# A streaming encoder layer: two more plain up-projection blocks, one weight cast moved to ScalarE, t1 kept in DRAM, and the closing norm's sums of x on VectorE

## What is computed

```python
h = x * (1 + sc2) + sh2
u = h @ w_up + b_up                     # 1024 -> 2 x 2816
ctx = concatenate([conv_buf, u], axis=1)
uc = conv_b + sum(conv_w[j] * ctx[:, j:j + T] for j in range(3))
a, g = split(uc, 2, axis=-1)
f = (a * gelu(g)) @ w_down              # 2816 -> 1024
x = layer_norm(ALPHA * x + g2 * f, ln2_w, ln2_b)
```

## Time and profile before

| | |
|---|---|
| median of 3 runs | 1892.29 us (1892.24 to 1895.44) |
| the profiled execution | 1895.71 us, its span 1893.9 us |
| TensorE busy | 1813.9 us, 96% of the span |
| VectorE, GpSimd, ScalarE busy | 1130.8, 862.4, 608.7 us |
| mean granted TensorE clock | 0.981 of full speed |
| chain that ended last | TensorE 84%, VectorE 6%, GpSimd, ScalarE and DMA 2% each |

### The profile page before, as it was taken

How to read it: one execution, slowest core, us unless ns; L and a number is a source line. 1 busy time by engine, 2 the same in 40 slices (tenths; PEclk the granted TensorE clock), 3 DMA queues, 4 the chain that set the end, 5 groups by cost and what they waited for, 6 DMA issues and landing times.

```text
span 1893.9 us, 30909 instructions
## 1 busy us (share of the span) xinstructions
PE 1813.9 (96%) x12255; PEld 1737.0 (92%) x12255; DVE 1130.8 (60%) x2002; ACT 608.7 (32%) x1375; POOL 862.4 (46%) x605
## 2 busy tenths in 40 slices
PE   7999999999999999999999996889999999999984
PEld 6999888888999999899999996889999999999983
DVE  4837875773322324364345869675676668666687
ACT  3213444433222323342111685122222222322345
POOL 0332212212222222133336357297778778877851
PEclk9999999999999999999999998899999999999997
DMA  9443321114334334265333001011111111101112
GB/s 389 167 145 107 120 85 69 57 57 136 97 107 125 123 107 121 84 230 182 125 125 102 12 12 49 23 46 45 45 46 68 39 53 45 68 23 68 45 34 83
DMA packets 78903, 173.44 MB, mean 92 GB/s; under 512 B 9300, under 2 KB 42452, under 8 KB 78632
## 3 DMA queue, kind: packets, MB, share of 16 engines
q1 hardware_dynamic: 55112, 119.63, 18.8%
q10 hardware_dynamic: 23648, 51.84, 7.7%
HBM read 139.21 MB, written 32.24 MB: 91 GB/s over the span
## 4 chain that ended last, share of the span: by engine, by line
PE 84%; DVE 6%; POOL 2%; ACT 2%; DMA 2%; DVEq 2%; issue 2%; ACTq 0%; SPq 0%; POOLq 0%
PE acc L607 37%; PE px L889 12%; PE acc L889 7%; PE px L935 6%; PE acc L935 4%; PE px L854 2%; PE px L678 1%; PE acc L854 1%; PE px L878 1%; PE px L707 1%; PE px L690 1%; PE px L704 1%; PE px L780 1%; PE px L779 1%; PE px L778 1%
## 5 line engine op out<-in xcount | busy, mean ns | idle before, releaser
L607 PE MATMUL acc<-x_hilo_a,w_hilo 128*128 128x352 f32 x4032 | 664.3, 324 | 2.6 <-ACT x_c L1037 1.7
L607 PEld LDWEIGHTS acc<-x_hilo_a,w_hilo 128*128 128x128 f32 x4032 | 643.1, 188 | 10.8 <-issue 10.0
L485 POOL CAST w_hilo<-w_raw 128x1024 fp32r<-128x1024 f32 x73 | 84.8, 1162 | 732.7 <-PE acc L607 624.8
L510 POOL TENSOR_TENSOR w_unit<-w_raw,w_unit 128x512 fp32r<-128x512 f32 x116 | 171.5, 1478 | 70.6 <-ACT w_unit L1371 61.7
L487 POOL TENSOR_TENSOR w_hilo<-w_raw,w_hilo 128x1024 fp32r<-128x1024 f32 x73 | 189.0, 2589 | 5.8
L935 PE MATMUL px<-ffn_act,w_unit 128*128 128x352 f32 x900 | 152.0, 324 | 0.6 <-issue 0.5
L935 PEld LDWEIGHTS px<-ffn_act,w_unit 128*128 128x128 f32 x900 | 145.6, 189 | 1.6 <-issue 1.4
L889 PE MATMUL px<-x_hilo_a,w_unit 128*128 128x264 f32 x1128 | 145.2, 284 | 0.2 <-POOL w_unit L510 0.2
L1774 DVE SCALAR_TENSOR_TENSOR c_state<-c_state,stage,px 128x257 f32<-128x257 f32 x36 | 17.4, 482 | 206.9 <-PE px L780 206.9
L889 PEld LDWEIGHTS px<-x_hilo_a,w_unit 128*128 128x128 f32 x1128 | 140.5, 188 | 0.3 <-issue 0.3
L889 PE MATMUL px<-h_sums,w_unit 128*128 128x264 f32 x828 | 109.2, 287 | 3.5 <-POOL w_unit L510 3.5
(11 more groups left out here) (319 smaller groups left out, 3037.4 us busy)
## 6 DMA issues: line engine op xcount, KB each, us to landing
w_raw<-in_w_panels SPq DMA_DIRECT2D x141, 512.0 KB, 3.3
z_spill<-stage ACTq DMA_DIRECT2D x41, 528.0 KB, 2.7
adaT_ring<-in_w_adaT SPq DMA_DIRECT2D x32, 512.0 KB, 4.5
stage<-z_spill ACTq DMA_DIRECT2D x20, 528.0 KB, 4.8
ada_ring<-in_w_ada SPq DMA_DIRECT2D x16, 512.0 KB, 13.3
zc<-z_spill SPq DMA_DIRECT2D x8, 1024.0 KB, 9.8
x_c<-in_x SPq DMA_DIRECT2D x8, 528.0 KB, 14.9
x_c<-in_x ACTq DMA_DIRECT2D x8, 528.0 KB, 4.0
```

The lines of the kernel that those rows point to most:

```text
L485: nc.gpsimd.tensor_copy(to[:, 0, :], raw[:, s, :]).then_inc(w_hi, 1)
L510: nc.gpsimd.tensor_tensor(to[:, 1, :], src, to[:, 0, :].bitcast(F32), ALU.subtract).then_inc(w_ready, 1)
L607: last = mm(acc[:, n, 0:NW], whl[:, slot, wi, k * P:(k + 1) * P], rhs[:, xi, k, n * NW:(n + 1) * NW], start=(k == 0 and j == 0), stop=(k = ...
```

## The change

- SINGLES takes in pi 3: eight plain blocks instead of six, and the first pair is pi 4 (PAIR0 = 4). Its order of terms is that of the others.
- The unit slots are handed out by the order in which the terms read them: a new unit takes the slot whose holder is read first (`unit_places`, UNIT_PREV). Of a pair, S4 now takes S2's slot (before: S1's), the next A11 takes S1's.
- ScalarE also casts the high half of A11 for each pair that doesn't follow a down-projection (even pi from 6 to 20, and 21), at the point of its queue between `x_take` of the pair before and `up_tap`. GpSimd waits for it on `a_hi`.
- t1 is no longer formed from XA. `sums_full` leaves it in h_full; ScalarE's queue stores it to DRAM after each `sums_high`, and loads it into XA's low part after the eighth block is taken. From the third on, `h2_full` waits until the first two stores have landed.
- The scaling of XC moves from VectorE to ScalarE, one row block at a time, with a semaphore on which VectorE's first down rows wait.
- The order of ScalarE's and VectorE's queues at the seam is another: `up_take(2)` stands ahead of the last `h2_full`.
- The closing norm's sums of x are formed by VectorE with `ln_add`, ahead of each `ln_add_square`; the loop at the end of GpSimd's program is gone.

```diff
-SINGLES = ((0, 0), (0, 1), (1, 0), (1, 1), (2, 0), (2, 1))
+SINGLES = tuple((pi, r) for pi in range(4) for r in range(2))
-PAIR0 = 3
+PAIR0 = 4
...
-        order += [("p", j, 1), ("p", j + 1, 0), ("d", j, 0), ("d", j, 1)]
+        order += [("p", j, 1)] * (j > 1) + [("p", j + 1, 0), ("d", j, 0), ("d", j, 1)]
...
-UNIT_SLOT = {unit: r % NUNIT for r, unit in enumerate(UNIT_RING)}
+def unit_places():
+
+    reads = [(item, part) for item in ITEMS[NSING:] for part in (terms(2 * item[1] + item[2]) if item[0] == "p" else (0, 1))]
+    slot, prev, held = {}, {}, {}
+    for r, unit in enumerate(UNIT_RING):
+        if r < NUNIT:
+            slot[unit], prev[unit] = r, None
+        else:
+            prev[unit] = min(held.values(), key=reads.index)
+            slot[unit] = slot[prev[unit]]
+        held[slot[unit]] = unit
+    return slot, prev
...
+        def after_down(pi):
+            return pi % 2 == 1 and PAIR0 < pi < 2 * FF - 2
+
+        def plain_parts(pi):
+            return ("A12", "A22") if pi == PAIR0 or after_down(pi) else ("A11", "A12", "A22")
...
-                if unit[1] in ("A12", "A22"):
-                    pool.wait_ge(a_hi, 2 * (2 * unit[0][1] + unit[0][2] - PAIR0) + (1 if unit[1] == "A12" else 2))
+                pi = 2 * unit[0][1] + unit[0][2]
+                if unit[1] in plain_parts(pi):
+                    pool.wait_ge(a_hi, high_of(pi, unit[1]))
...
+            split(P_FFN + 6)
+            split(P_FFN + 7)
...
-            for n in range(NT):
-                cols = slice(n * NW, (n + 1) * NW)
-                for m in range(1, KT - 2 if n == NT - 1 else KT):
-                    pool.wait_ge(r_rdy, rank(1, m, n) + 1)
-                    if m > 1:
-                        pool.wait_ge(s1_add, (KT - 1) * (NT + n) + m - 1)
-                    nc.gpsimd.tensor_tensor(lsum2[:, 0, cols], XC[:, 0, cols] if m == 1 else lsum2[:, 0, cols], XC[:, m, cols], ALU.add)\
-                      .then_inc(s1_add, 1)
...
+            def t1_store(kt):
+                act.dma_start(io["t1"][kt], hb[:, kt % 2, 0, 0:HN]).then_inc(ffn_dma, 16)
+
+            def t1_load(kt):
+                act.dma_start(XA[:, 1, kt, HN:T].bitcast(F32), io["t1"][kt]).then_inc(ffn_dma, 16)
...
             def h2_full(kt):
                 if kt >= 2:
                     act.wait_ge(ts_lo, kt - 1)
                     act.wait_ge(t34_lo, kt - 1)
+                    act.wait_ge(ffn_dma, 16 * 3)
...
+            def residual_scale(k):
+                A(XC[:, k, :], XC[:, k, :], ACT.Identity, scale=der[:, 4, k:k + 1], bias=der[:, 5, k:k + 1]).then_inc(xc_rdy, 1)
...
             sums_high(1)
+            up_take(1, 2)
             h2_full(2)
-            up_take(1, 2)
-            h2_full(3)
             up_tap(0, 1)
-            sums_high(2)
-            sums_high(3)
             for n in range(NT):
                 up_take(2, n)
+            h2_full(3)
+            sums_high(2)
             up_tap(1, 0)
+            sums_high(3)
             ffn_gelu(0)
...
+            for n in range(NT):
+                up_take(7, n)
+            for kt in range(KH):
+                t1_load(kt)
+            up_tap(3, 1)
             for kt in range(KH):
                 t1_high(kt)
...
                 if pi > PAIR0:
+                    if not after_down(pi):
+                        plain_high(pi, "A11")
                     up_tap(pi - 1, 1)
                     up_tap(pi - 1, 0)
...
             def down_row(j, m):
+                if j == 0:
+                    dve.wait_ge(xc_rdy, m + 1)
...
+            down_row(0, 0)
+            conv_first(3, 0)
+            down_row(0, 1)
+            t1_low(0)
+            t1_low(1)
             dve.drain()
-            conv_second(2, 1)
-            down_row(0, 1)
-            t1_full(0)
+            conv_second(3, 0)
             down_row(0, 2)
...
                     down_take(("t", m, n))
+                    if m and not (n == NT - 1 and m >= KT - 2):
+                        ln_add(1, m, n)
```

More of the change, by code:

```diff
@@ L95, with terms @@
 UNIT_RING = [unit for unit in UNITS if unit[0][0] == "p" or unit[0][1] < FF - 1]
-UNIT_SLOT = {unit: r % NUNIT for r, unit in enumerate(UNIT_RING)}
+def terms(pi):
+    return "A11", "S2", "S1", "S3", "A12", "A22", "S4"
+def unit_places():
[9 more added lines that the diff above has]
+    return slot, prev
+UNIT_SLOT, UNIT_PREV = unit_places()
+LAST_SINGLE = {SLOT[P_FFN + i]: i for i in range(NSING)}
 def bank_fills():
@@ L365, in part_of, with high_of @@
             return 6 * (pi - PAIR0) + 2 * ("U2", "U3", "C22").index(part) + q + 1
+        def after_down(pi):
+            return pi % 2 == 1 and PAIR0 < pi < 2 * FF - 2
+        def plain_parts(pi):
+            return ("A12", "A22") if pi == PAIR0 or after_down(pi) else ("A11", "A12", "A22")
+        def high_of(pi, part):
+            return sum(len(plain_parts(x)) for x in range(PAIR0, pi)) + plain_parts(pi).index(part) + 1
         def row_made(pi, r):
@@ L370, in unit_free @@
         def unit_free(eng, unit):
-            r = UNIT_RING.index(unit)
-            if r < NUNIT:
-                eng.wait_ge(*ready(("u", *SINGLES[3 + r // 2], NT - 1)))
+            if UNIT_PREV[unit] is None:
+                eng.wait_ge(*ready(("u", *SINGLES[LAST_SINGLE[UNIT_SLOT[unit] // 2]], NT - 1)))
                 return
-            item, part = UNIT_RING[r - NUNIT]
+            item, part = UNIT_PREV[unit]
             if item[0] == "d":
@@ L1370, in plain_high @@
                 unit_free(act, (item, part))
-                A(wu[:, UNIT_SLOT[item, part], 0, :], raw[:, p % 2, HALF:D], ACT.Copy).then_inc(a_hi, 1)
+                A(wu[:, UNIT_SLOT[item, part], 0, :], raw[:, p % 2, 0:HALF] if part == "A11" else raw[:, p % 2, HALF:D], ACT.Copy).then_inc(a_hi, 1)
             def x_take(pi):
@@ L1485, in _ @@
             up_tap(1, 1)
+            for k in range(4):
+                residual_scale(k)
             act.wait_ge(t34_lo, KH)
             act.wait_ge(ts_lo, KH)
+            act.wait_ge(ffn_dma, 16 * (KH + 1))
             ffn_round(0)
@@ L1491, in _ @@
             ffn_gelu(1)
+            up_tap(2, 0)
             ffn_round(1)
[L1493 removed]
             for n in range(NT):
@@ L1496, in _ @@
             up_tap(2, 1)
-            act.dma_start(fcr[:, :, :, :], io["ffn_consts"]).then_inc(fc_in, 16)
+            act.dma_start(fcr[:, :, :, :], io["ffn_consts"]).then_inc(ffn_dma, 16)
+            for k in range(4, KT):
+                residual_scale(k)
+            for n in range(NT):
+                up_take(6, n)
+            ffn_gelu(2)
+            up_tap(3, 0)
+            for n in range(NT):
+                up_take(7, n)
+            for kt in range(KH):
+                t1_load(kt)
+            up_tap(3, 1)
             for kt in range(KH):
                 t1_high(kt)
-                if kt == 1:
-                    ffn_gelu(2)
-            act.wait_ge(fc_in, 32)
+            ffn_gelu(3)
+            plain_high(PAIR0, "A12")
             for pi in range(PAIR0, 2 * FF):
                 if pi > PAIR0:
+                    if not after_down(pi):
+                        plain_high(pi, "A11")
                     up_tap(pi - 1, 1)
                     up_tap(pi - 1, 0)
-                if pi % 2 and PAIR0 < pi < 2 * FF - 2:
-                    ffn_gelu(pi - 1)
-                plain_high(pi, "A12")
+                    if after_down(pi):
+                        ffn_gelu(pi - 1)
+                    plain_high(pi, "A12")
                 first_take(pi)
                 plain_high(pi, "A22")
-                if not (pi % 2 and pi < 2 * FF - 2):
+                if pi == PAIR0:
+                    ffn_round(2)
+                elif not after_down(pi):
                     ffn_gelu(pi - 1)
@@ L1918, in sums_full @@
                 V.tensor_tensor(h2[:, 0:HN], h2[:, 0:HN], h2[:, HN:T], ALU.subtract).then_inc(ts_rdy, 1)
-            def residual_scale(kt):
-                for k in (kt, kt + KH):
-                    V.tensor_scalar(XC[:, k, :], XC[:, k, :], der[:, 4, k:k + 1], der[:, 5, k:k + 1], ALU.mult, ALU.add)
             def t2_low(kt):
```

72 lines of the change are left out of this document (27 added, 45 removed).

## The result

The changed kernel took 1902.49 us (median of 5 runs, 1900.88 to 1903.87), beside 1892.98 us for the kernel before (5 runs on the same chip, 1892.24 to 1895.44): a ratio of 1.0045, 95% interval 1.0032 to 1.0059, that is +9.5 us. It is slower, as forecast (1897.9), and 4.6 us more than the number given. It lies inside the range 1883 to 1904, and 0.5 us above the 1895 to 1902 that the forecast allowed itself. The profiled execution took 1902.49 us with a span of 1900.7; against the 1893.9 of before that is +6.8.

What follows compares the result with a forecast made beforehand. TensorE alone was taken to bound the repeated part, with idle time at the seam and tail. -26.0 + 20.8 + 10.2 + 0.5 + 0.1 = +5.6 us on 1892.3 gave 1897.9 us, range 1883 to 1904.

Steps and rivals of the forecast that it cites:

- The even pairs: Pairs 6 to 20: ScalarE's late A11 cast delays S2, so TensorE waits 2.6 us in each of eight, +20.8 us.
- the lower bound of 0.7 us: Even pairs: the wait for S2 if its cast and low half don't collide with VectorE's convolution.
- 1.7 for six of the eight: Even pairs: the clock falls in six of eight gaps, costing 1.7 us each, +10.2 us (0 to 14).
- 4.68 where 2.92 is normal: Time of 24 matmuls after the old 3.48 us gap, read as a clock loss of 1.75 us.
- The rival in which the clock holds: Even pairs: the clock holds in most gaps, -10.2 us or part of it, 1888 to 1894 us; chance 0.23.
- The seam: Attention's end to first FFN groups: fifth block's wait ends, sixth waits some 6 us, d1 starts at 1238.5, -26.0 us.
- Stores ... land in 2.7 us; issued at 1132: Seam: h2_full(2) waits for two stores to DRAM, which let it start near 1134.6.
- The loads of t1: Seam: four loads issued at 1195.3, landing by 1201 at worst, ahead of VectorE's third down row; costed at nothing.
- +0.5: Pair 21: S2 ready some 0.8 us later, half of which the clock may give back, +0.5 us (0 to 1).
- GpSimd waited for its panel anyway: Pair 21: the reason given for the late A11 cast costing only +0.5 us there.
- does not help: Even pairs: S4's new slot, free 2.9 us earlier, gains nothing because A11 is held up by ScalarE.
- a difference carries over unchanged: Profile to median: the +5.6 us is added to the median of 1892.3, giving 1897.9 us.

Runs made afterwards that it cites:

- the third experiment: The changed kernel with ScalarE's cast of A11 placed between the two halves of x_take: 1873.77 us, ratio 0.9882 to the kernel before.
- the base: The changed kernel with A11's high half made by GpSimd again in every pair: 1867.19 us, ratio 0.9848 to the kernel before.
- the last kernel: The base with sixth panel's split ahead of sums_low, fifth's between the first two, and four residual scalings ahead of the tap: 1858.68 us, ratio 0.9809.
- the last two kernels: The base with four residual scalings ahead of the tap and both splits ahead of sums_low (1861.42 us), or the fifth's between the first two (1858.68 us).

## Why the prediction was right, and where it was off

- **The even pairs: right, term by term.** The working said A11's low half 0.9 us behind ScalarE's cast (1274.29 to 1275.21), S2's sum, cast and low half in a row, the cast beside VectorE's convolution, 2.6 us. It was 2.62 in each. Taking the cast back gave 35 us (37 by the ratios), putting it into the old kernel cost 33. The choice that mattered was to take the collision at full size and not the lower bound of 0.7 us: S2's cast took 1.52 us for 0.61 and its low half 2.16 for 1.29, and the third experiment gets back the cast's 0.9.
- **The clock in those gaps.** The step "1.7 for six of the eight" came out near in its sum by two misses that offset each other: all eight fell, and each cost 1.45 us (4.07 less 2.62; against the base, whose groups are 0.2 us shorter than those of the kernel before, it is 1.68), +11.6 for +10.2. The 1.7 rests on "4.68 where 2.92 is normal", which sets a row's length against a distance between starts; a row of 24 is 3.09 long, so that fall cost 1.6. The rival in which the clock holds did not come.
- **The seam: the mechanism right, two sizes off, 2.4 us too little gain.** That the fifth block's wait ends was not quite so: 1.50 us are left, for GpSimd's split, but the sum runs over the sixth block and doesn't hang on it. The step "Stores ... land in 2.7 us; issued at 1132" failed: they were issued 6 and 2 us earlier and nothing waited for them, so the sixth block's panel was ready 1.6 us sooner (1156.78 for 1158.4). And the clock behind that gap cost 1.5 us (72 matmuls in 13.10 for 11.6) instead of 2.4. That is luck and no miss: behind the same gap (4.1 to 4.7 us) the 72 took 12.99 to 14.53 us in the six kernels of the experiments that have it, 1.4 to 2.9 us lost. The loads of t1 were hidden, as costed: ScalarE had them at 1198.08, VectorE used them from 1199.73.
- **Pair 21: the step "+0.5" was too small, +2.2.** The cast stood behind x_take of pair 20, which ran at 1777.15, and GpSimd began A11 at 1778.79 although its panel should have been there from 1775.7, an estimate from the base, where GpSimd began 3.46 us behind the sum that frees the place (1739.55 to 1743.01). Two sums then ran beside VectorE (2.16 us for 1.29). "GpSimd waited for its panel anyway" was true of the kernel before, and not of the changed one, where it waited 4.44 us for ScalarE.
- **The slots: "does not help" was right for the changed kernel.** Its groups are as long as with old slots (68.20 and 68.19 us). Where A11 is on time the new ones gain 0.2 us per group.
- **From the profile to the median.** The step "a difference carries over unchanged" failed by 2.7 us. The profiled execution of before stood 3.4 us above its median and that of after on its own, and single executions of one kernel lie up to 5 us apart (1891.9 to 1896.95 for the kernel before on one chip). One source of it is seen in code that the change doesn't touch, below. What else went into the 2.7 us was not taken apart.

## What to carry to other kernels

A cast handed to a less busy engine is only as early as the instruction ahead of it in that engine's queue: read what that instruction waits for before looking at busy shares. Here the same cast cost 35 us behind a take and 1.3 us ahead of it. When a stage is full to 99.8%, as the groups were, any unit made later than its term is paid in full and once per repetition, while a large gain at a seam is had only once. And a change that bundles several edits is worth taking apart: without one of them it was 1.5% faster, and three edits to the next waits in line at the seam gave another 0.4%, most of it by the first two.

## What the runs showed of the hardware

- **An idle gap of the same length may or may not lower the clock.** Behind 1.71 us of idle TensorE at the first norm, in code that is the same in all kernels, the first 24 matmuls took 4.29 us in the base, at a granted clock of 1.00, and 5.57 in the last kernel, at 0.50 at first (rows of 1097.18 and 1098.11). Over the fourteen profiles they took 4.24 to 4.29 us in six and 5.28 to 6.66 in eight. Behind the 2.74 us of pair 21 they took 3.16 in the base, and 4.39 and 5.62 in the last two kernels. But the gaps of 2.62 us in the even pairs lowered it every time, 18 of 18 in three kernels; sixteen of these come 68.2 us after one another in two kernels, so they are not eighteen independent trials. What decides is not shown. The Trainium skill ("TensorE: Matmul & The Clock Gate", section "Why this matters for your kernels") warns of drops only for idle gaps longer than any of these. The traces disagree. From them a gap of 1.7 us or more has to be costed with a chance of a fall, and 1.0 to 2.5 us for it.
- **A DMA in ScalarE's queue was issued before the instructions ahead of it had run** where no semaphore stood between: each of the four stores stands behind three casts and was issued beside the first of them (1126.35 beside 1126.34, the third cast starting at 1127.42). It reads data that those casts don't write, so nothing is wrong in it, but the issue time of such a DMA is not the end of what precedes it.
- **GpSimd's cast of 128 x 512 took 0.61 us alone and 1.52 beside VectorE's convolution**, and the convolution 2.13 at 1280.26 where it took 1.33 at 1411.21 in the third experiment. This agrees with the Trainium skill ("SBUF — State Buffer", section "SBUF: two separate sides"), by which GpSimd and a VectorE operation with two SBUF inputs, as this one is, share one pair of ports that one instruction holds as a whole.
